# Stacked rounded parts for the score products of a second attention, split at the stage's begin

## The reference, cut to what matters

```python
ss = jnp.einsum('bqgjd,bgqnkd->bgjqnk', qb, kg).astype(jnp.float32) * scale   # selected blocks
ps = jax.nn.softmax(jnp.where(valid_s, ss, NEG_INF), axis=-1)
sw = jnp.einsum('bqgjd,bkgd->bgjqk', qb, kwb).astype(jnp.float32) * scale      # window
pw = jax.nn.softmax(jnp.where(valid_w, sw, NEG_INF), axis=-1)
o = gb[..., 0:1] * o_c + gb[..., 1:2] * o_s + gb[..., 2:3] * o_w
```

## Time and profile before

| | us |
|---|---|
| median of 3 runs | 3558.97 (3558.35 to 3563.8) |
| the profiled execution, its own time | 3559.45 |
| its span | 3557.5 |
| TensorE busy | 3466.9 (97% of the span) |
| VectorE busy | 2320.5 (65%) |
| ScalarE busy | 1452.2 (41%) |
| GpSimd busy | 396.9 (11%) |

### The profile page before, as it was taken

How to read it: one execution, slowest core, us unless ns; L and a number is a source line. 1 busy time by engine, 2 the same in 40 slices (tenths; PEclk the granted TensorE clock), 3 DMA queues, 4 the chain that set the end, 5 groups by cost and what they waited for, 6 DMA issues and landing times. The chain is left out here.

```text
span 3557.5 us, 45948 instructions
## 1 busy us (share of the span) xinstructions
PE 3466.9 (97%) x17381; PEld 2885.4 (81%) x17388; DVE 2320.5 (65%) x4206; ACT 1452.2 (41%) x2425; POOL 396.9 (11%) x312
## 2 busy tenths in 40 slices
PE   8999999999999899999999999999999999999998
PEld 6776778999999878888877767788888776778886
DVE  6656766889899798898844556554334555654433
ACT  4343343433899534333333234433223323443221
POOL 1000000000233335333210000100001000010000
PEclk9999999999999999999999999999999999999999
DMA  4321243545899999999722224333332222423332
GB/s 149 101 71 43 74 139 105 195 169 171 273 367 373 372 346 400 400 384 390 293 84 83 76 83 143 101 102 99 95 95 89 80 73 86 156 91 101 95 94 72
DMA packets 213166, 597.28 MB, mean 168 GB/s; under 512 B 22258, under 2 KB 80404, under 8 KB 211412
## 3 DMA queue, kind: packets, MB, share of 16 engines
q1 hardware_dynamic: 176084, 460.13, 38.7%
q0 software_dynamic: 36864, 134.23, 9.8%
HBM read 523.36 MB, written 69.21 MB: 167 GB/s over the span
## 5 line engine op out<-in xcount | busy, mean ns | idle before, releaser
L580 ACT ACTIVATE stream_hi<-stream_raw 128x1024 fp32r<-128x1024 f32 (+1 forms) x611 | 639.0, 1046 | 1050.0 <-PE ffn_ps L2861 411.3
L588 DVE TENSOR_TENSOR stream_lo<-stream_raw,stream_hi 128x1024 fp32r<-128x1024 f32 (+1 forms) x607 | 734.4, 1210 | 441.8 <-ACT stream_hi L580 437.2
L622 PE MATMUL experts_ps<-h_hi,stream_hi 128*128 128x384 f32 x1024 | 346.7, 339 | 1.1 <-PEq L752 1.1
L622 PE MATMUL experts_ps<-h_lo,stream_hi 128*128 128x384 f32 x1024 | 342.2, 334 | 0.0
L622 PE MATMUL experts_ps<-h_hi,stream_lo 128*128 128x384 f32 x1024 | 342.2, 334 | 0.0
L1181 PE MATMUL experts_ps<-stream_hi,mix_a_hi 128*128 128x512 f32 x768 | 300.3, 391 | 17.4 <-issue 15.6
L1181 PE MATMUL experts_ps<-stream_hi,mix_a_lo 128*128 128x512 f32 x768 | 300.2, 391 | 0.0
L1181 PE MATMUL experts_ps<-stream_lo,mix_a_hi 128*128 128x512 f32 x768 | 300.1, 391 | 0.0
L2859 PE MATMUL mid_ps<-h_hi,stream_hi 128*128 128x512 f32 x672 | 275.4, 410 | 3.8 <-PEq L3101 2.2
L2859 PE MATMUL ffn_ps<-h_hi,stream_hi 128*128 128x512 f32 x704 | 275.1, 391 | 0.2 <-DVE h_lo L2926 0.2
L2860 PE MATMUL ffn_ps<-h_lo,stream_hi 128*128 128x512 f32 x704 | 273.9, 389 | 0.0
(11 more groups left out here) (519 smaller groups left out, 6863.4 us busy)
## 6 DMA issues: line engine op xcount, KB each, us to landing
stream_raw<-u SPq DMA_DIRECT2D x128, 512.0 KB
stream_raw<-v SPq DMA_DIRECT2D x128, 512.0 KB
stream_raw<-l_gu SPq DMA_DIRECT2D x88, 512.0 KB
expert_hidden<-experts_gelu SPq DMA_DIRECT2D x128, 192.0 KB
expert_weights<-built SPq DMA_DIRECT2D x12, 2048.0 KB
built<-expert_weights SPq DMA_DIRECT2D x16, 1536.0 KB, 14.3
stream_raw<-l_gate SPq DMA_DIRECT2D x48, 512.0 KB
built<-expert_hidden SPq DMA_DIRECT2D x124, 192.0 KB
```

What stands on the lines that cost most here:

```text
L580: self.nc.scalar.activation(self.hi[n % self.RING][:, 0:w], self.raw[n % self.RAW][:, 0:w], ACT.Copy).then_inc(self.hi_done, 1)
L588: self.nc.vector.tensor_tensor(self.lo[n % self.RING][:, 0:w], self.raw[n % self.RAW][:, 0:w], self.hi[n % self.RING][:, 0:w].bitcast(F32) ...
L622: mm = self.nc.tensor.matmul(self.ps[n % 2], a, b[:, k, :], start=(k == 0 and m == 0), stop=(k == DC - 1 and m == 2))
```

## The change

The score products no longer take the f32 queries and keys from `z`. Queries and keys are split into a rounded part (high) and the rest (low), both fp32r, and are laid out so that one product over 128 rows takes high and low part of a head's queries against the rounded keys, which stand twice, one copy on each half of the partitions. A second product over 64 rows takes the high part of the queries against the low part of the keys. So a head and bank has two products instead of one, and a pair eight instead of four.

The 14 places for the parts lie over the chunks 6 to 19 of `z`: three for each set of keys (head 0 doubled, head 1 doubled, low parts) and two for each chunk of queries. The split is made inside the stage:

- `scalar(-1)` and `scalar(0)`: before and behind the exponentials of pair 0 ScalarE rounds columns 0 to 255 and 256 to 511 of the first queries (2 instructions) and both sets of keys (4 each), 10 instructions on 64 partitions by 256 columns each time; `vector(-1)` and `vector(0)`, ahead of the largest of pair 0 and behind its weighing, make the rests by 6 instructions each time.
- `scalar(1)`, `(5)`, `(9)`: the rounding of the next chunk's queries, 2 instructions of 512 columns; `vector(2)`, `(6)`, `(10)`: its rest, 2 instructions.
- TensorE waits for these ahead of the scores of pairs 0, 2, 4, 8 and 12.
- `GateAhead`: the first half of gate 0 (12 products) now goes ahead of the scores of pair 0, and the second half stands where the whole gate stood.

The other two callers of `paired_attention` pass `Whole()`, which adds nothing.

```diff
+class Stacks:
+    UPPER, LOWER = slice(0, 64), slice(64, 128)
...
+    def queries_high(self, q, to, cols=slice(0, SEQ)):
+        S = self.nc.scalar
+        S.activation(to[0][self.UPPER, cols], q[self.UPPER, cols], ACT.Copy)
+        return S.activation(to[1][self.LOWER, cols], q[self.LOWER, cols], ACT.Copy)
+
+    def queries_low(self, q, to, cols=slice(0, SEQ)):
+        V = self.nc.vector
+        V.tensor_tensor(to[0][self.LOWER, cols], q[self.UPPER, cols], to[0][self.UPPER, cols].bitcast(F32), ALU.subtract)
+        return V.tensor_tensor(to[1][self.UPPER, cols], q[self.LOWER, cols], to[1][self.LOWER, cols].bitcast(F32), ALU.subtract)
+
+    def keys_high(self, k, to, cols=slice(0, SEQ)):
+        S = self.nc.scalar
+        for u, rows in enumerate((self.UPPER, self.LOWER)):
+            for place in (self.UPPER, self.LOWER):
+                ins = S.activation(to[u][place, cols], k[rows, cols], ACT.Copy)
+        return ins
+
+    def keys_low(self, k, to, cols=slice(0, SEQ)):
+        V = self.nc.vector
+        for u, rows in enumerate((self.UPPER, self.LOWER)):
+            ins = V.tensor_tensor(to[2][rows, cols], k[rows, cols], to[u][rows, cols].bitcast(F32), ALU.subtract)
+        return ins
+
+    def parts(self, q_to, k_to, at, keys):
+        own = (self.UPPER, self.LOWER)
+        return [([q_to[u][:, at] for u in range(2)], [k_to[u][:, keys] for u in range(2)]),
+                ([q_to[u][own[u], at] for u in range(2)], [k_to[2][own[u], keys] for u in range(2)])]
...
                     if n >= AHEAD:
                         pe.wait_ge(exp_done, SIDES * (n - AHEAD + 1))
+                    split.tensor(pe, n)
                     for bank, parts, width in pairs[n].products:
...
+                beside.ahead(pe)
                 for n in range(AHEAD):
                     score(n)
...
+                split.vector(dve, -1)
                 largest(0)
                 for n in range(N):
                     weigh(n)
+                    split.vector(dve, n)
...
+                split.scalar(act, -1)
                 exps(0)
+                split.scalar(act, 0)
...
                     if n + 1 < N:
                         exps(n + 1)
+                        split.scalar(act, n + 1)
...
+class GateAhead(GatesByPair):
+    def ahead(self, pe):
+        self.half(pe, 0, 0)
+    def tensor(self, pe, n):
+        if n == 0:
+            self.half(pe, 0, 1)
+        else:
+            GatesByPair.tensor(self, pe, n)
+
+class StacksBesideGates(Stacks):
+    HALVES = (slice(0, SEQ // 2), slice(SEQ // 2, SEQ))
...
+    def tensor(self, pe, n):
+        if n in (0, 2, 4, 8, 12):
+            pe.wait_ge(self.low, (0, 2, 4, 8, 12).index(n) + 1)
+    def scalar(self, act, n):
+        if n in (-1, 0):
+            cols = self.HALVES[n + 1]
+            self.queries_high(self.q[0], self.q_to[0], cols)
+            self.keys_high(self.k[0], self.k_to[0], cols)
+            self.keys_high(self.k[1], self.k_to[1], cols).then_inc(self.high, 1)
+        if n in (1, 5, 9):
+            pair = n // 4 + 1
+            self.queries_high(self.q[pair], self.q_to[pair]).then_inc(self.high, 1)
+    def vector(self, dve, n):
+        if n in (-1, 0):
+            cols = self.HALVES[n + 1]
+            dve.wait_ge(self.high, n + 2)
+            self.queries_low(self.q[0], self.q_to[0], cols)
+            self.keys_low(self.k[0], self.k_to[0], cols)
+            self.keys_low(self.k[1], self.k_to[1], cols).then_inc(self.low, 1)
+        if n in (2, 6, 10):
+            pair = n // 4 + 1
+            dve.wait_ge(self.high, pair + 2)
+            self.queries_low(self.q[pair], self.q_to[pair]).then_inc(self.low, 1)
...
-                    products=[(512 * j, [(q, [z[rows, of, 0:w] for rows in halves])], w) for j, of in enumerate((Z_KS, Z_KW))],
+                    products=[(512 * j, split.parts(split.q_to[n], split.k_to[j], at, slice(0, w)), w) for j in range(2)],
```

More of the change, by code:

```diff
@@ L199, in __init__, with rounded_over, begin, paired_attention @@
         self.extra, self.values, self.dst = extra, values, dst
-def paired_attention(nc, name, C, pairs, scale, cols, places, beside, by_scalar, lead):
+def rounded_over(nc, name, before, tiles, side=None):
+    with ExitStack() as stack:
+        if before:
+            stack.enter_context(nc.sbuf_tensor(f"{name}_before", [P, before, SEQ], F32, side=side))
+        return stack.enter_context(nc.sbuf_tensor(name, [P, tiles, SEQ], F32R, side=side))
+class Whole:
+    def begin(self, st, scored):
+        pass
+    def tensor(self, pe, n):
+        pass
+    def scalar(self, act, n):
+        pass
+    def vector(self, dve, n):
+        pass
+class Stacks:
+    UPPER, LOWER = slice(0, 64), slice(64, 128)
+    def __init__(self, nc):
+        self.nc = nc
+    def queries_high(self, q, to, cols=slice(0, SEQ)):
[21 more added lines that the diff above has]
+                ([q_to[u][own[u], at] for u in range(2)], [k_to[2][own[u], keys] for u in range(2)])]
+def paired_attention(nc, name, C, pairs, scale, cols, places, beside, by_scalar, lead, split):
     N, SIDES, WIDE, RING = len(pairs), 2, 4 * P, 3
@@ L225, in paired_attention @@
         beside.begin(st)
+        split.begin(st, scored)
         def copied_after(g):
@@ L1394, in half, with ahead, __init__, begin @@
             self.gates.tensor(pe, self.slots[n], range(which * DC // 2, (which + 1) * DC // 2))
+class GateAhead(GatesByPair):
+    def ahead(self, pe):
+        self.half(pe, 0, 0)
[6 more added lines that the diff above has]
+    HALVES = (slice(0, SEQ // 2), slice(SEQ // 2, SEQ))
+    def __init__(self, nc, z, places):
+        Stacks.__init__(self, nc)
+        self.q = [z[:, Z_Q + n, :] for n in range(NSA_PAIRS)]
+        self.k = [z[:, of, :] for of in (Z_KS, Z_KW)]
+        self.k_to, self.q_to = [places[3 * j:3 * j + 3] for j in range(2)], [places[6 + 2 * n:8 + 2 * n] for n in range(NSA_PAIRS)]
+    def begin(self, st, scored):
+        self.high, self.low = st.sem("stack_high"), st.sem("stack_low")
+    def tensor(self, pe, n):
+        if n in (0, 2, 4, 8, 12):
+            pe.wait_ge(self.low, (0, 2, 4, 8, 12).index(n) + 1)
+    def scalar(self, act, n):
+        if n in (-1, 0):
[6 more added lines that the diff above has]
+            self.queries_high(self.q[pair], self.q_to[pair]).then_inc(self.high, 1)
+    def vector(self, dve, n):
+        if n in (-1, 0):
[8 more added lines that the diff above has]
+            self.queries_low(self.q[pair], self.q_to[pair]).then_inc(self.low, 1)
 def pool_and_gla(nc, name, C, y, values, w_a2, w_pool, scale, m, head_root, bank, gates):
@@ L2549, in dilated @@
                 dst=y_dil[:, n, at]))
-    paired_attention(nc, "dil", C, pairs, HD ** -0.5, 768, wide_places(ps), beside, 2, False)
+    paired_attention(nc, "dil", C, pairs, HD ** -0.5, 768, wide_places(ps), beside, 2, False, Whole())
 def first_constants(shared, const1, masks):
@@ L2567, in attention_part @@
         bank = [ps[:, cols] for cols in slices(8, 512)]
+        z_rounded = rounded_over(nc, "z_rounded", Z_DIL, Z_CHUNKS - Z_DIL)
         z = sb("z", [P, Z_CHUNKS, SEQ])
@@ L2585, in attention_part @@
         dilated(nc, C, masks, z, v_tok, v4_tok, [slice(r, SEQ, 4) for r in range(4)], y_dil, ps, beside)
-        pairs, halves = [], (slice(0, 64), slice(64, P))
+        pairs, split = [], StacksBesideGates(nc, z, [z_rounded[:, j, :] for j in range(Z_CHUNKS - Z_DIL)])
         for n in range(NSA_PAIRS):
@@ L2589, in attention_part @@
                 w, at = (t + 1) * P, slice(t * P, (t + 1) * P)
-                q = [z[rows, Z_Q + n, at] for rows in halves]
                 pairs.append(Pair(
-                    products=[(512 * j, [(q, [z[rows, of, 0:w] for rows in halves])], w) for j, of in enumerate((Z_KS, Z_KW))],
+                    products=[(512 * j, split.parts(split.q_to[n], split.k_to[j], at, slice(0, w)), w) for j in range(2)],
                     masks=[(512, 512 * j + t * P, masks["causal"]) for j in range(2)], parts=[(0, w), (512, w)],
@@ L2598, in attention_part @@
         paired_attention(nc, "nsa", C, pairs, HD ** -0.5, 1024, wide_places(ps),
-                         GatesByPair(merge_gates, {n: n for n in range(N_MERGE_GATES)}), 0, True)
+                         GateAhead(merge_gates, {n: n for n in range(N_MERGE_GATES)}), 0, True, split)
 def up_and_out(nc, name, C, stream, y_nsa, y_dil, x, gains, h_hi, h_lo, x_rstd, gate_dram, gate_stored, next_bank):
@@ L3621, in latent_attention @@
                 values=[(s * P, v[:, s, P * i:P * i + P]) for s in range(t + 1)], dst=y[:, Y_CQ + i, at]))
-    paired_attention(nc, name, C, pairs, MLA_QK ** -0.5, SEQ, places, beside, 0, True)
+    paired_attention(nc, name, C, pairs, MLA_QK ** -0.5, SEQ, places, beside, 0, True, Whole())
 def program(nc, A, out):
```

## The result

The changed kernel takes 3577.24 us (median of 5 runs, 3576.8 to 3581.47), the kernel before in the same job 3560.17 (3558.35 to 3572.02). The ratio is 1.0041, with a 95% interval from 1.0025 to 1.0057: slower, by less than half a percent. The profiled execution took 3576.8 us, its span is 3574.7 against 3557.5: 17.2 more.

What follows compares the result with a forecast made beforehand. TensorE, busy 97% of the span, was taken to bound the kernel, with the engine chain counting at the begin. Splits 4.6 plus scores 5.7 gave +10.3 us on 3559.45, 3569.8; less 0.5 for the median, 3569.3 us; range 3561 to 3576.

Steps and rivals of the forecast that it cites:

- the changes of row mode: Score products of pairs 2 to 15: switching between 128 and 64 rows costs drain plus bare load, +5.7 us in all.
- the splits at the begin: Stage's begin: the roundings and subtractions of both column halves delay pair 2's scores, +4.6 us.
- the later splits: Pairs 1, 2, 5, 6, 9 and 10: roundings and subtractions fit into waits, cost nothing; 3.9 us without that cover.
- The first rival: Score products: weight loads pulled ahead over mode changes, so only a pair's edges pay; not slower, 3560.9 us, chance 0.15.
- the second: Rival at 128-column score products: narrow fp32r takes four passes, 3.8 us more, 3573.1 us, chance 0.25.
- the fourth: Rival: splits at the begin cost only 2.5 us, 3567.2; with changes at 0.15 us, 3564.7; chance 0.1.
- so 0.31 each: Begin's splits: ScalarE's back-to-back roundings of 256 columns overlap and take 0.31 us each, ten 3.1 us.
- the 0.33 of VectorE: Begin's splits: VectorE's subtractions of 256 columns overlap alike and take 0.33 us in a row, six 2.0 us.
- bound of 7.5: Begin's splits: upper bound of their cost, 7.5 us, if the instructions don't overlap.
- the third rival: Stage's begin: waits bring TensorE to 1.2 GHz again after pair 2's scores begin, 3.5 us more, 3572.8, chance 0.15.
- The half gate ahead: Ahead of pair 0's scores: half of gate 0 fills 2.8 us, so TensorE idles 2.5 us there.

Runs made afterwards that it cites:

- 1: Changed kernel with a pair's products over 128 rows of both banks first, then those over 64: 3571.66 us, 1.0032 to the kernel before.
- experiment 2: Changed kernel with the second product of each head and bank over all 128 rows too: 3575.01 us, 1.0037 to the kernel before.
- experiment 10: Changed kernel with the ten roundings ordered by the partition halves they read and write: 3575.91 us in one run, stage 190.4 against 193.3.
- 7: Changed kernel with six roundings over 128 partitions per half of the columns, key-doubling copies left out: 3571.92 us, 1.0043 to the kernel before.
- 8: Changed kernel with VectorE's second half of the split and gate piece behind pair 1's largest: 3573.81 us, 1.004 to the kernel before.
- 9: Changed kernel with the whole gate 0 behind pair 1's scores, nothing ahead of pair 0's: 3580.36 us, 1.0062 to the kernel before.
- 4: Changed kernel with the earlier f32 score products; splits, waits and half gate ahead stay: 3570.79 us, 1.0018 to the kernel before.
- experiment 6: Kernel before, no splits, with the first half of gate 0 between the scores of pairs 0 and 1: 3556.07 us, 0.9989 to the kernel before.

## Why the prediction was right, and where its sizes were off

Its direction was right, and so was its reason: both of its terms, the changes of row mode and the splits at the begin, are there, and the later splits are hidden. TensorE idles 8.4 us in the stage, about 8 forecast. But the stage is 17.6 us longer, not 10.3. The median, 3577.24, is 7.9 above the forecast and 1.2 above the range. The kernel before was slower in that job as well (3560.17); the 3558.97 that the forecast started from times the ratio is 3573.6, within the range.

- **Changes of row mode.** Forecast 2.11, 1.79, 1.47 and 1.23 us for a pair's block, measured 2.18, 1.86, 1.49 and 1.25. Experiments 1 and 2 show that it is the changes and neither array time nor the number of loads; a part of each change is a load with nothing beside it, as forecast. The sum of +5.7 for pairs 2 to 15 came to 5.4 from pair 3 on, 0.4 in pair 2 and 0.3 behind pair 15's scores. The first rival (loads pulled ahead) fell with the gaps between the loads above, the second (four passes at 128 columns) with the 1.25 us, and the fourth (cheap splits, changes at 0.15 us) with the splits' length and the 0.19.
- **The splits at the begin** were the term that was mis-sized: +4.6 forecast, +8.6 measured to pair 2's scores. The step that failed is "so 0.31 each", and the 0.33 of VectorE: both engines start the split's instructions 0.43 apart (4.26 us for ten, 2.6 for six). The two halves of the columns take 6.9 and 6.7 us where 5.3 and 5.4 were forecast, 3.0 us more. The pace was taken from instructions that stay on the same partitions, and the split goes from one half to the other each time; for ScalarE experiment 10 shows this, for VectorE no run changes the order. The trace of before has a row for it, which the prediction does not use: VectorE's eight instructions of 64x256 in an earlier stage, four on one half and then four on the other. The first line here holds the third and fourth, the second the fifth:

```profile
157.63 0.74 DVE L2489 TENSOR_TENSOR rope_pairs<-y_dil,rope_pe 64x256 f32<-64x256 f32 x2
...
158.39 0.42 DVE L2489 TENSOR_TENSOR rope_pairs<-y_dil,rope_pe 64x256 f32<-64x256 f32 x1
```

  The fourth starts at 157.63 + 0.74 - 0.41 = 157.96, the fifth, on the other half, 0.43 later. The prediction's bound of 7.5 for instructions that don't overlap was nearly the case itself: 8.6 less the 1.0 that follows.
- **The slow clock.** From pair 0's scores to the largest it takes 1.6 us longer than before (302.74 - 300.04 against 294.52 - 293.44), forecast 0.6: the scores run at 1.2 GHz. And the third rival came true beside the forecast, not instead of it: the clock is back at 2.4 GHz near 312.7 and falls again near 316, so that pair 2's scores and the first quarter of gate 1 run at 1.2 GHz. Of the +3.3 from pair 2's scores to pair 3's 0.4 are the products and 2.9 the clock, since experiments 7, 8 and 9 take 10.57 us for the same products at 2.4 GHz, against 13.51; the rival had 3.5. The prediction gave it 0.15 as if it excluded the forecast. Which wait goes with the second fall is seen across the runs. It is TensorE's wait for pair 0's turned block, ahead of the scores of pair 2:

| kernel | that wait | pair 2's scores to pair 3's |
|---|---|---|
| 7, 9 | none | 10.57 |
| 8 | 0.3 | 10.57 |
| changed | 1.2 | 13.51 |
| 10 by halves | 1.7 | 12.06 |
| 2, 4 | 2.9 | 11.76, 11.84 |
| 1 | 3.2 | 11.62 |

  In the five runs with a wait of 1.2 to 3.2 us the clock fell behind it, in the three with 0.3 us or none it did not; how long it stayed down differs, and 1, 2 and 4 have other products. That the wait is the cause is likely, but no experiment changed the wait alone.
- **The later splits** were hidden, as said: experiment 4 has them and loses nothing from pair 4 on.
- **The half gate ahead** was taken as filling 2.8 us of wait. It did, but the chain beside it needed none of that time, and without it the profiled stage is 3.0 us shorter.

Between the 10.3 forecast and the 17.6 measured lie 3.0 for the splits, 1.0 and 2.9 for the slow clock, and 0.4 in the products.

## What to carry to other kernels

Count the changes between products over 128 and over 64 rows before counting passes: here a change cost 0.19 us, nearly as much as a whole fp32r product of 512 columns (0.23), and two heads side by side in f32 were cheaper than the rounded products that took their place (1.92 against 2.18 us at 512 columns). Work put in front of a stage's first product lies on the chain through all engines, whatever TensorE does beside it; the better place for filling work was the wait that was there already, behind the first scores (experiment 6, without the splits). When two costs follow from one wait, add them, and don't hand them out to rivals.

## What the runs showed of the hardware

- Instructions of 256 columns on 64 partitions start 0.31 to 0.33 us apart on ScalarE and 0.33 to 0.34 on VectorE while they stay on one half of the partitions, and 0.41 to 0.43 where the next one reads or writes another half; over all 128 partitions ScalarE's start 0.31 apart. A record's own length is the same 0.40 to 0.42, so behind a change of half the next one starts when the last has ended, or nearly.
- fp32r products of 128 columns do not take four passes: eight of them over 128 rows took 0.95 us (experiment 2). The changed kernel's block of 1.25 us fits one pass (1.23 in the prediction's sum; two would make it 1.45, an estimate by the same sum).
- TensorE's clock fell while TensorE was busy: in the changed kernel it was 1.00 from 312.8 to 316.0 us, with waits of 1.2 and 0.5 us in it, and 0.50 from 316.2 to 322.8 us, in which TensorE never idled. In experiment 9, without the 1.2 us wait, it was 1.00 from 310.2 to 323.0.
